# Eight PSUM banks shared out differently: three banks in turn for the projection steps, two for all transposes of the attention stage

## The reference, cut to what matters

```python
z = h @ w_in                        # h: the RMS-normed input, 1088 x 1024
q, k, v, gate_a, f_logit, u, vb, gate_b, g_a, g_b = split(z)
q = rms_norm(q, q_norm_g)           # per head, 8 heads of 64
k = rms_norm(k, k_norm_g)
logf = log_sigmoid(f_logit + b_forget)
c = cumsum(logf)
s = q @ k.T * HEAD_DIM ** -0.5 + (c[:, None] - c[None, :])   # per head, causal
p = softmax(s)
attn = p @ v
...
m = sigmoid(g_a) * (a @ w_pa) + sigmoid(g_b) * (b @ w_pb)
```

## Time and profile before

| | |
|---|---|
| runs, median (lowest to highest) | 2304.95 us (2304.56 to 2306.32), 3 runs |
| the profiled execution | 2303.95 us, its span 2302.3 us, mean granted TensorE clock 0.949 |
| busy share, whole span | PE 88%, PEld 80%, DVE 43%, ACT 30%, POOL 21% |
| attention stage, layer 1 | about 64 to 606 us of the span |
| attention stage, layer 2 | about 1183 to 1737 us of the span |

### The profile page before, as it was taken

The page is one execution under the profiler, slowest core; times in us unless marked ns, Lnnn a source line. Parts: engine busy times, 40 slices in busy tenths (PEclk is TensorE's granted clock), DMA queues, the critical chain, the costliest instruction groups (busy, mean ns, idle before and its releaser), DMA issues. The chain is left out here.

```text
span 2302.3 us, 32930 instructions
## 1 busy us (share of the span) xinstructions
PE 2020.2 (88%) x11560; PEld 1848.3 (80%) x11560; DVE 981.4 (43%) x2344; ACT 695.8 (30%) x1515; POOL 493.2 (21%) x508
## 2 busy tenths in 40 slices
PE   2779999999785999897967999999988689989898
PEld 2769999999565889895847899999986578989776
DVE  3324454554463334444424354454444442434343
ACT  3233343433332222103213334343333232221122
POOL 0432333331102112202015133333201110121110
PEclk9989999999897999998978999999999799999899
DMA  5241132311214322423222223132112142225221
GB/s 164 59 107 51 48 95 53 92 53 45 66 32 111 96 69 58 149 92 131 89 66 69 81 54 90 51 80 62 38 37 74 42 141 79 62 73 171 102 96 64
DMA packets 216900, 183.62 MB, mean 80 GB/s; under 512 B 50164, under 2 KB 186884, under 8 KB 216724
## 3 DMA queue, kind: packets, MB, share of 16 engines
q1 hardware_dynamic: 216724, 181.39, 27.3%
HBM read 132.17 MB, written 49.17 MB: 79 GB/s over the span
## 5 line engine op out<-in xcount | busy, mean ns | idle before, releaser
L71 PE MATMUL bank<-keep_hhi,at_fhi 128*128 128x384 f32 (+1 forms) x768 | 261.8, 341 | 34.0 <-POOL at_flo L738 29.9
L72 PE MATMUL bank<-keep_hlo,at_fhi 128*128 128x384 f32 (+1 forms) x768 | 253.6, 330 | 0.0
L73 PE MATMUL bank<-keep_hhi,at_flo 128*128 128x384 f32 (+1 forms) x768 | 253.4, 330 | 0.0
L71 PE MATMUL bank<-keep_hhi,br_whi 128*128 128x384 f32 (+1 forms) x576 | 201.0, 349 | 42.2 <-POOL br_wlo L997 21.2
L71 PE MATMUL bank<-at_whi,keep_hhi 128*128 128x384 f32 (+3 forms) x576 | 200.9, 349 | 26.3 <-POOL at_wlo L733 25.9
L72 PE MATMUL bank<-at_wlo,keep_hhi 128*128 128x384 f32 (+3 forms) x576 | 197.6, 343 | 0.0
L73 PE MATMUL bank<-at_whi,keep_hlo 128*128 128x384 f32 (+3 forms) x576 | 197.3, 342 | 0.0
L72 PE MATMUL bank<-keep_hlo,br_whi 128*128 128x384 f32 (+1 forms) x576 | 193.5, 336 | 0.0
L73 PE MATMUL bank<-keep_hhi,br_wlo 128*128 128x384 f32 (+1 forms) x576 | 193.2, 335 | 0.0
L696 ACT ACTIVATE at_prob<-at_prob,at_nmx 128x128 f32<-128x128 f32 (+7 forms) x128 | 99.5, 777 | 276.2 <-DVE at_nmx L876 276.2
L71 PEld LDWEIGHTS bank<-keep_hhi,at_fhi 128*128 128x128 f32 x768 | 146.3, 190 | 37.8 <-issue 30.4
(11 more groups left out here) (234 smaller groups left out, 4605.2 us busy)
## 6 DMA issues: line engine op xcount, KB each, us to landing
mg_gate<-gates SPq DMA_DIRECT2D x32, 544.0 KB, 6.7
at_stage<-in_w_in SPq DMA_DIRECT2D x128, 128.0 KB, 2.5
at_stage<-in_w_in SPq DMA_DIRECT2D x64, 192.0 KB, 2.5
gates<-at_th SPq DMA_DIRECT2D x64, 192.0 KB, 2.3
br_stage<-in_w_in SPq DMA_DIRECT2D x48, 256.0 KB, 3.2
at_decay<-ncum SPq DMA_DIRECT2D x16, 512.0 KB, 4.0
br_k<-in_cache_k SPq DMA_DIRECT2D x32, 256.0 KB, 3.0
br_v<-in_cache_v SPq DMA_DIRECT2D x32, 256.0 KB, 2.9
```

Of the source, the lines that this page charges most:

```text
L71: nc.tensor.matmul(out, sh, mh, start=start and i == 0, stop=False)
L72: nc.tensor.matmul(out, sh, ml, start=False, stop=False)
L73: last = nc.tensor.matmul(out, sl, mh, start=False, stop=stop and i == n - 1)
```

## The change

The bank of X joins the banks of Z and P, so that Z and P take turns in three banks, and each Z or P waits for the user three places before it. X and T steps share the two banks of T, taking turns in the order of the list: each X or T waits for the second user before it, whichever kind that is. The waits follow (`wait_bank` now serves all four kinds). The list of steps, the copies out of PSUM and every other wait are the same.

```diff
-    zps, sps, tps, ops, xps = g.bank[0:2], g.bank[2:4], g.bank[4:6], g.bank[6], g.bank[7]
+    zps, sps, tps, ops = (*g.bank[0:2], g.bank[7]), g.bank[2:4], g.bank[4:6], g.bank[6]
...
         if s[0] == "Z" or s[0] == "P" and s[3] == 0:
-            bank_of[s] = len(users) % 2
-            if len(users) >= 2:
-                bank_before[s] = users[-2]
+            bank_of[s] = len(users) % 3
+            if len(users) >= 3:
+                bank_before[s] = users[-3]
             users.append(s)
+    turned = []
+    for s in plan:
+        if s[0] in "TX":
+            bank_of[s] = len(turned) % 2
+            if len(turned) >= 2:
+                bank_before[s] = turned[-2]
+            turned.append(s)
...
             if u[0] == "Z":
                 eng.wait_ge(z_free, order[u] + 1)
+            elif u[0] == "T":
+                eng.wait_ge(t_lo, order[u] + 1)
+            elif u[0] == "X":
+                eng.wait_ge(x_hi, order[u] + 1)
+                eng.wait_ge(x_lo, xlo_before[u])
             else:
                 eng.wait_ge(p_taken, 3 * u[1] + u[2] + 1)
 
     def bank(s):
-        return zps[bank_of[s]]
+        return (tps if s[0] in "TX" else zps)[bank_of[s]]
...
                     pe.wait_ge(qn_r, zi + 1)
-                    if xi:
-                        pe.wait_ge(x_hi, xi)
-                        pe.wait_ge(x_lo, xlo_before[s] - (t < PT_))
+                    wait_bank(pe, s)
...
                     pe.wait_ge(p_ready, order[("S", h, 4 * G + 3)] + 1)
-                    if ti >= 2:
-                        pe.wait_ge(t_lo, ti - 1)
+                    wait_bank(pe, s)
```

More of the change, by code:

```diff
@@ L676, in _ @@
                         nc.scalar.activation(qk[:, slots(p), :, t * P:(t + 1) * P],
-                                             xps[:, :].rearrange("p (s h r) -> p h s r", s=2, h=2),
+                                             bank(s)[:, :].rearrange("p (s h r) -> p h s r", s=2, h=2),
                                              ACT.Copy).then_inc(x_hi, 1)
                     else:
-                        both = xps[:, :].rearrange("p (s h r) -> p s h r", s=2, h=2)
+                        both = bank(s)[:, :].rearrange("p (s h r) -> p s h r", s=2, h=2)
                         nc.scalar.activation(g.qk_s[0:HD, :, p, :], both[0:HD, :, 0, 0:NS_TOK], ACT.Copy)
@@ L705, in _ @@
                         act.wait_ge(v_done, ti - LAG)
-                    nc.scalar.activation(pt_hi[:, ti % (LAG + 1), lo:512], tps[ti % 2][:, lo:512], ACT.Copy).then_inc(t_hi, 1)
+                    nc.scalar.activation(pt_hi[:, ti % (LAG + 1), lo:512], bank(s)[:, lo:512], ACT.Copy).then_inc(t_hi, 1)
                 elif kind == "O":
@@ L884, in _ @@
                     dve.wait_ge(t_hi, ti + 1)
-                    nc.vector.tensor_tensor(pt_lo[:, ti % (LAG + 1), lo:512], tps[ti % 2][:, lo:512],
+                    nc.vector.tensor_tensor(pt_lo[:, ti % (LAG + 1), lo:512], bank(s)[:, lo:512],
                                             pt_hi[:, ti % (LAG + 1), lo:512].bitcast(F32), ALU.subtract).then_inc(t_lo, 1)
@@ L936, in _ @@
                             at = (2 * i + j) * P
-                            last = nc.tensor.transpose(xps[:, at:at + n],
+                            last = nc.tensor.transpose(bank(s)[:, at:at + n],
                                                        qn[0:n, 2 * i + hh, :, :].rearrange("p e d -> p (e d)"),
@@ L972, in _ @@
                     pe.wait_ge(p_ready, order[("S", h, 4 * G + 3)] + 1)
-                    if ti >= 2:
-                        pe.wait_ge(t_lo, ti - 1)
+                    wait_bank(pe, s)
                     for r in range(first, 4):
                         at = blk(4 * G + r) + j * P
-                        last = nc.tensor.transpose(tps[ti % 2][:, r * P:(r + 1) * P], prob[:, at:at + P], g.ident[:, :])
+                        last = nc.tensor.transpose(bank(s)[:, r * P:(r + 1) * P], prob[:, at:at + P], g.ident[:, :])
                     last.then_inc(t_ready, 1)
```

## The result

| | before | changed |
|---|---|---|
| median of 6 runs each | 2306.57 us | 2318.36 us |
| lowest to highest | 2304.56 to 2312.16 | 2316.12 to 2321.10 |
| ratio | | 1.0049, 95% interval 1.0035 to 1.0063 |
| profiled execution | 2303.95 us | 2320.95 us |

The change makes the kernel 0.5% slower: 11.3 us by the ratio, 8 to 15 us by its interval. The forecast was 12.1 us.

A forecast was written before the change was run, and what follows sets the result against it. TensorE's pauses were taken to bound the attention stage: -4.2 removed, +15.3 added and +1.0 for the clock gave +12.1 us on 2303.95, so 2316.1, and a median of 2317.0 us (+0.5%), range 2311 to 2326.

The forecast's parts named there:

- What bounds the stage: Attention stage, both layers: TensorE is fed without a break, idle only 45 and 50 us of 542 and 554 us.
- By nothing else: The end of the stage moves only by what is added to or taken from TensorE's pauses.
- What is removed: Pauses before P(1,0,0) and P(2,0,0) go with the third bank: 2.10 us in each layer, 4.2 us gained.
- Both pauses of E: P(1,0,0) starts 1.42 us late and P(2,0,0) 0.68 us late, waiting for the tanh of E; both go.
- The pause of P(10,1,0): 0.73 us before this step goes, but V(4,0,0) then pauses 0.73 us longer; value 0.
- What is added: T steps wait for the last DVE read of an X two turns before: 7.63 us a layer, 15.3 us in all.
- the six steps: T(1,0,1), T(2,1,3), T(4,1,3), T(3,0,3), T(3,1,1), T(5,1,1): new pauses of 1.09, 1.22, 1.22, 1.66, 0.78, 1.66 us.
- T(1,0,2): Would wait for the read of T(1,0,1), but moves back 1.09 us with that step's pause; value 0, otherwise 0.75 us a layer.
- The clock: Lower granted clock after long TensorE pauses: 1.0 us added, two thirds of one 1.6 us loss, for four 1.66 us pauses.
- The third bank does win: Answers the rival that the third bank wins nothing at P(1,0,0) and P(2,0,0): +16.3 us, 2321 us, chance 0.13.
- The lower clock: Rival: each of twelve new pauses brings the lower clock, 19 us beside the 11.1, 2335 us, chance 0.08.
- The swallowing of the pauses: Rival: existing waits before X(p,8) and V(4,0,0), 6.2 us a layer, swallow the pauses; 2303.6 us, chance 0.05.

The follow-up runs named there:

- the ring: Z, P, T and X take turns in one ring of five banks, each waiting for the user five places before, against the kernel before: ratio 0.9981.
- a turn of three: X and T take turns in three banks, Z and P in two, against the kernel before: ratio 0.9994.
- DVE's order: The changed kernel, but DVE does its share of X(p,t-1) ahead of its share of Z(p,t): ratio to the kernel before 1.0031.
- X read twice: The changed kernel, but DVE does X's last subtraction twice for t up to 7: ratio to the kernel before 1.0104.
- the sharing alone: The changed kernel, but Z and P go back to two banks and the eighth bank is unused: ratio to the kernel before 1.0067.
- X(p,8) later: The kernel before, but X(p,8) of the second to fourth pair stands two T places later in the list: ratio 0.9977.

## Why the prediction was right, point by point

- **What bounds the stage.** Right for the change. All engines but TensorE are busy as long as before, and the time came from TensorE's pauses. "By nothing else" was too strong: the granted clock moves the stage by as much, and of the pauses taken away elsewhere (X(p,8)) more than half came back.
- **What is removed.** Right. Both pauses of E went, 2.10 us in a layer, in every kernel with a third bank for Z and P or the ring, and stayed in those without. The pause of P(10,1,0) was given back at V(4,0,0): 0.92 us in layer 1, and 0.29 + 0.73 = 1.02 was expected. In layer 2 only 0.28 us went and 0.61 came, which the prediction, made from layer 1, did not have; it is 0.3 us.
- **What is added.** Right at each of the six steps, in both layers: 1.14, 1.27, 1.26, 1.60, 0.74, 1.65, together 7.66 us against 7.63. No other T paused that did not before. T(1,0,2), let go because it moves back with the pause before it, did not wait (read over at 248.88 + 0.55 = 249.43, start at 249.89), and did wait once that pause was short. The cause was shown from three sides: a turn of three takes the pauses away and the time with them, DVE's order shrinks them, a longer read lengthens them and the time.

```profile
248.88 0.55 DVE L897 TENSOR_TENSOR at_ptlo<-bank,at_pthi 128x384 fp32r<-128x384 f32 x1
...
249.89 0.25 PEld L986 LDWEIGHTS bank<-keep_ident,at_prob 128*128 128x128 f32 x2
```

- **The clock.** The weak term. The 1.0 us for pauses of 1.66 us has nothing to show for it: in this profile no lower clock follows any of the twelve new pauses, nor in the one with X read twice, where they reach 2.25 us. After X(p,8), 1.97 us, it follows at 3 of 6 places (2 before). The prediction also missed a case in its own trace. In layer 2 of the kernel before, two pauses at S steps, 1.47 and 0.81 us, stand before a stretch at about half the clock, and in layer 1 the same pauses do not:

```profile
1296.00:1299.20 3.20, 1.40 (x7) 1.09 (x7) 2.67 (x10) 0.93 (x3) 0.00 (x0) 1.00 0.01 3
1299.20:1302.70 3.50, 3.07 (x10) 2.38 (x9) 3.34 (x11) 2.16 (x4) 0.00 (x0) 0.51 0.00 0
```

So the length of a single pause does not tell whether the clock falls after it. Without the term the forecast is 11.1 us, and the interval, 8 to 15 us, can't tell the two. That the total came within 1 us of the measured one is therefore in part luck; what is not luck are the pauses. Of the Trainium skill's rule on idles from cycling through PSUM banks ("TensorE: Matmul & The Clock Gate", section "A second HAM failure mode: psum-queue depth-cycling"), the trace of the changed kernel shows nothing at pauses of this size and number. The Trainium skill's rule that all eight banks be used ("Perfetto Trace Analysis", section "Matmul Optimizations") did not decide either: the sharing alone leaves one unused and costs 15.5 us, but the kernels that use all eight lie between 5.3 us below and 24 us above the kernel before, by the ratio.

- **The rivals.** The third bank does win (old pauses back in the sharing alone). The lower clock did not follow the new pauses. The swallowing of the pauses did not happen, since X(p,8) still waits its 1.97 us. V(2,0,0) swallowed 0.3 us in layer 1 and 0.2 us in layer 2.

## What to carry to other kernels

Before banks are shared out anew, take for each step the end of the read that frees its bank in the new turn, and compare it with the start of the step in the trace of the old kernel. A list of waits shows only what already hurts; this comparison gave each new pause to 0.1 us. Where steps of different kinds share a ring, it is the turn's length against the slowest read in it that counts: the same sharing cost 15 us with a ring of two and nothing with three or five. The comparison has to be made again when the list changes: with X(p,8) later, the ring of five got a pause of 0.74 us in each layer. A pause that is taken away on the bounding engine is worth its length only up to the next wait whose release does not come sooner with it.

## What the runs showed of the hardware

The mean granted clock of the same kernel differed from run to run, from 0.943 to 0.951 among 29 runs of the kernel before on one core, and the time with it, from 2318.8 us at the lowest clock to 2300.2 us at the highest. That is 0.8%, more than this change. A lower clock need not come right behind a pause. In a stretch outside the changed stage, where TensorE is busy throughout, the profiled execution of the changed kernel was granted 0.85:

```profile
880.00:903.00 23.00, 23.00 (x126) 22.36 (x126) 9.25 (x21) 5.38 (x13) 3.27 (x3) 0.85 0.26 66
```

It was busy throughout the 20 us before it too, at 1.00. The kernel before was granted 1.00 in this part of the code (865 to 890 us of its span).
